# A streaming encoder layer on 8 cores: weights laid out in blocks, cast in one DMA each, scratch stores spread over three tiles, sample tokens worked beside the first and the last tile

## The reference, cut to what matters

```python
def trunk_layer(x, ..., cache_k, cache_v):
    h = rms_norm(x, n_pre_mix)
    z = h @ w_in                                   # 1024 x 5632
    q, k, v, zg, ga, gb = jnp.split(z, offs, axis=-1)
    a = attn_prompt(q, k, v, sinks)                # own 64-frame chunk + 2 before
    # or attn_sample(q, k, v, cache_k, cache_v, sinks)
    u, gv = jnp.split(jax.nn.gelu(zg), 2, axis=-1)
    gv = layer_norm(gv, ln_g, ln_b)
    bm = spatial_gate(u, gv, w_s, b_s)             # u * (tril(w_s) gv + b_s), 128 positions
    merged = sigmoid(ga) * (a @ w_attn_proj) + sigmoid(gb) * (bm @ w_gmlp_proj)
    x = x + rms_norm(merged @ w_out, n_post_mix)
    h2 = rms_norm(x, n_pre_ffn)
    g, up = jnp.split(h2 @ w_ffn_in, 2, axis=-1)   # 1024 x 5632
    x = x + rms_norm((silu(g) * up) @ w_ffn_out, n_post_ffn)
    return x, new_k, new_v, gv
```

## Time and profile before

| what | value |
|---|---|
| three runs, us | 4579.6, 4606.01, 5141.87 (median 4606.01) |
| profiled execution, us | 4594.15 |
| its span on the slowest core (core 5), us | 4592.5 |
| spans of the eight cores, us | 4560.1 to 4592.5 |
| granted clock, mean of a core | 0.969 to 0.971 |
| busy: PE, DVE, ACT, POOL | 91%, 45%, 40%, 25% |
| DMA queues: SyncE's (q1), GpSimd's (q0) | 605.81 MB, 95.31 MB (as written) |

### The profile page before, as it was taken

One profiled execution on the slowest core, in us unless ns is written; L12 is line 12 of the kernel. 1 busy time (PEld: TensorE's weight loads), 2 busy tenths in 40 slices (PEclk: granted clock), 3 DMA queues, 4 the chain that ended last, 5 costly groups with the idle time before them and its releaser, 6 DMA issues.

```text
span 4592.5 us, 64392 instructions; the slowest of 8 cores (4560.1 to 4592.5 us)
## 1 busy us (share of the span) xinstructions
PE 4193.3 (91%) x21528; PEld 1887.5 (41%) x21528; DVE 2054.6 (45%) x2957; ACT 1848.6 (40%) x3525; POOL 1166.0 (25%) x1225
## 2 busy tenths in 40 slices
PE   2549899989999999999999999999999999999895
PEld 1214344434444444444444444444444444444343
DVE  1425445445454445445354445445454545445322
ACT  1515335243443526343353525344353525344231
POOL 1111022222223222232323222232323223232322
PEclk8779999989999999999999999999999999999997
DMA  6749953515435353533535343533535353543357
GB/s 120 152 84 201 209 187 120 181 63 187 160 121 187 135 168 140 178 130 125 187 112 197 133 173 138 179 129 127 188 111 198 131 179 129 173 137 131 133 184 263
DMA packets 168453, 709.43 MB, mean 154 GB/s; under 512 B 31073, under 2 KB 76129, under 8 KB 98498
## 3 DMA queue, kind: packets, MB, share of 16 engines
q1 hardware_dynamic: 87314, 605.81, 38.2%
q0 software_dynamic: 79088, 95.31, 10.0%
q10 hardware_dynamic: 1728, 4.20, 0.3%
HBM read 670.39 MB, written 69.99 MB: 161 GB/s over the span
## 4 chain that ended last, share of the span: by engine, by line
PE 73%; DMA 12%; DVE 6%; issue 4%; POOL 3%; ACT 2%; DVEq 0%; ACTq 0%; POOLq 0%; SPq 0%
PE ps L314 72%; DMA ring<-w_in 3%; DVE tmpf L342 3%; DMA ring<-wfi 2%; DMA yp<-tmpf 2%; DMA ring<-wap 2%; DVE hst L342 2%; POOL stt L331 1%; PE ps L482 1%; DVE xt L331 1%; ACT junk L321 1%; POOL big L331 1%; DMA ring<-s_wfi 1%; DMA wsf<-w_s 0%; DVE stt L338 0%
## 5 line engine op out<-in xcount | busy, mean ns | idle before, releaser
L314 PE MATMUL ps<-big,ring 128*128 128x512 bf16 (+1 forms) x12784 | 2745.0, 371 | 194.1 <-DMA ring<-w_in 51.2
L314 PEld LDWEIGHTS ps<-big,ring 128*128 128x128 bf16 x12784 | 1176.0, 99 | 1634.3 <-issue 344.6
L314 PE MATMUL ps<-ring,big 128*128 128x512 bf16 (+2 forms) x5476 | 1163.8, 371 | 24.0 <-POOL big L331 12.5
L331 POOL TENSOR_TENSOR big<-tmpf 128x512 bf16<-128x512 f32 (+1 forms) x480 | 603.8, 1258 | 1453.6 <-ACT tmpf L326 1152.1
L319 ACT ACTIVATE big<-ps 128x512 bf16<-128x512 f32 (+2 forms) x674 | 437.6, 658 | 916.0 <-PE ps L314 507.2
L314 PEld LDWEIGHTS ps<-ring,big 128*128 128x128 bf16 (+1 forms) x5476 | 531.9, 98 | 608.4 <-issue 47.1
L331 POOL TENSOR_TENSOR stt<-stt,negh 128x1 f32<-128x1 f32 (+1 forms) x297 | 226.9, 765 | 1297.7 <-DVE stt L335 913.7
L342 DVE SCALAR_TENSOR_TENSOR tmpf<-tmpf,ps 128x512 f32<-128x512 f32 (+1 forms) x374 | 245.7, 657 | 654.2 <-ACT tmpf L319 638.1
L319 ACT ACTIVATE y<-ps 64x512 bf16<-64x512 f32 (+2 forms) x1024 | 488.5, 478 | 54.0 <-ACT y L319 0.7
L321 ACT ACTIVATE junk<-ps 128x512 bf16<-128x512 f32 x260 | 155.1, 597 | 729.7 <-PE ps L314 722.3
L639 DVE RECIPROCAL dent<-dent 128x256 f32<-128x256 f32 (+1 forms) x264 | 441.8, 1693 | 8.3 <-DVE dent L331 0.5
(11 more groups left out here) (93 smaller groups left out, 1890.5 us busy)
## 6 DMA issues: line engine op xcount, KB each, us to landing
ring<-s_win SPq DMA_DIRECT2D x176, 1024.0 KB, 6.1
ring<-s_wfi SPq DMA_DIRECT2D x176, 1024.0 KB, 5.0
ring<-s_wfo SPq DMA_DIRECT2D x64, 1024.0 KB, 5.0
ring<-s_wap SPq DMA_DIRECT2D x32, 1024.0 KB, 10.0
ring<-s_wgp SPq DMA_DIRECT2D x32, 1024.0 KB, 10.8
ring<-s_wout SPq DMA_DIRECT2D x32, 1024.0 KB, 5.1
yp<-tmpf POOLq DMA_DIRECT2D x120, 256.0 KB, 9.0
xt<-xp POOLq DMA_DIRECT2D x52, 512.0 KB, 11.9
```

What stands on the lines that cost most here:

```text
L314: m.op(PE, lambda e: e.matmul(out, lhsT=lhsT, rhs=rhs, start=start, stop=stop), reads=reads, writes=[("ps", b)])
L331: m.op(eng, lambda e: e.tensor_tensor(out=out, in0=in0, in1=in1, op=op), reads=reads, writes=writes)
```

## The change

The host lays each weight out in blocks of [128, 8, 512] (with the head order of q and of wap's rows, and the g and u halves of wfi's blocks, already in place). A block is cast by one DMA, whose row for a partition is one run of 16 KB of f32. Scratch has one contiguous MB per block. A block is cast from f32 not only at its first use: `store_use` says at which use (0 is tile 0) the slot is stored as well, and only later uses load from scratch. The PX and YQ switch moves from the end of iteration 0 to that of iteration 2. The sample tile leaves the loop. Its own small buffers (`bigs`, `tmps`, `kTs`, `Vts`) let its qkv, u, gv and gates run beside tile 0's in the prologue, on the same ring slots (`smp["w"] = t["w"]`), and its merge, wout and feed-forward beside tile 15's. Constants are loaded in two parts, `consts_a` behind the first norm and `consts_b` in the middle of tile 0's u; w_s comes transposed from the host, so `setup_wmt` and `sample_w` are gone.

```diff
-        for h in range(16):
-            t, half = qperm(h)
-            cb, j = divmod(t, 4)
-            c0 = j * 128 + half * 64
-            cj(("s_win", cb), (A_, A_, slice(c0, c0 + 64)), wsrc(w_in, h * 64, 64))
...
         for cb in range(11):
+            reg(("s_win", cb), w_in[cb, :, :, :], s_win[cb, :, :, :], 1 + cb % 2)
+            reg(("s_wfi", cb), wfi[cb, :, :, :], s_wfi[cb, :, :, :], 1 if cb < 4 else 2)
         for cb in range(2):
+            reg(("s_wap", cb), wap[cb, :, :, :], s_wap[cb, :, :, :], 1)
+            reg(("s_wgp", cb), wgp[cb, :, :, :], s_wgp[cb, :, :, :], 1)
+            reg(("s_wout", cb), wout[cb, :, :, :], s_wout[cb, :, :, :], 1)
             for c, (k0, k1) in enumerate(FCH):
+                reg(("s_wfo", cb, c), wfo[cb, :, k0:k1, :], s_wfo[cb, :, k0:k1, :], 2)
...
-            if key not in converted:
-                converted.add(key)
-                for idx, in_ in conv_jobs[key]:
-                    m.dma(POOL, ("ring0", s), slot_v[idx], in_, writes=[("ring", s)])
-                m.dma(SP, ("cvst", key), blk_view[key], slot_v, reads=[("ring", s)], writes=[key])
+            n = uses.get(key, 0)
+            uses[key] = n + 1
+            if n <= store_use[key]:
+                m.dma(POOL, ("ring0", s), slot_v, f32_of[key], writes=[("ring", s)])
+                if n == store_use[key]:
+                    m.dma(SP, ("cvst", key), b16_of[key], slot_v, reads=[("ring", s)], writes=[key])
             else:
-                m.dma(SP, ("ring", s), slot_v, blk_view[key], reads=[key], writes=[("ring", s)])
+                m.dma(SP, ("ring", s), slot_v, b16_of[key], reads=[key], writes=[("ring", s)])
...
         for b in range(4):
             xload(SP, tiles[0], b)
+        m.dma(SP, ("c_g", 0), gS[:, 0, :], g_in[0][0:1, :].partition_broadcast(128), writes=[("gS", 0)])
+        xload(SP, smp, 0)
...
+        m.fence([POOL], [k for b in range(4) for k in xk(b)])
+        for s_ in range(2):
+            m.dma(POOL, ("c_ck", s_), ckb[:, s_, :], ck[s_, :, :], writes=[("ckb", s_)])
+            m.dma(POOL, ("c_cv", s_), Vc[:, s_, :], cv[s_, :, :], writes=[("Vc", s_)])
+        def consts_a():
+            m.fence([SP], BK(tiles[0], C_H, C_H + 8, (3,)))
+            m.dma(SP, "c_es", es[:], sinks[0:1, :].partition_broadcast(128), writes=["es"])
...
+        def consts_b():
+            m.fence([SP], BK(tiles[0], C_U, C_U + 4, ALLB))
+            for i in range(1, 4):
+                m.dma(SP, ("c_g", i), gS[:, i, :], g_in[i][0:1, :].partition_broadcast(128), writes=[("gS", i)])
+                act(gS[:, i, :], gS[:, i, :], AF.Copy, [("gS", i)], [("gS", i)], scale=32.0)
+            for b in range(4):
+                xload(SP, tiles[1], b)
...
+        both(qkv_units(t)[0:10], qkv_units(smp)[0:10], 10)
+        both(qkv_units(t)[10:], qkv_units(smp)[10:], 4)
...
+        both(u_units(t)[0:4], u_units(smp)[0:4], 4)
+        ev(now[0], consts_b)
+        both(u_units(t)[4:], u_units(smp)[4:], 4)
...
+            if fin:
+                for f in range(8):
+                    for second in (False, True):
+                        dense(merge_unit(smp, f, second), SC)
+                for n in range(2):
+                    dense(wout_unit(smp, 0, n), UNIT)
+                plan_post(smp, 0, now[0])
...
+            for c in range(13 if fin else 11):
+                if c < 11:
+                    ffn_col(t, c, UNIT)
+                if fin and c >= 2:
+                    ffn_col(smp, c - 2, SC)
-            if i == 0:
+            if i == 2:
                 ev(now[0] + 2.5 + UNIT, lambda: (PX.__setitem__(0, POOL), YQ.__setitem__(0, POOL)))
```

More of the change, by code:

```diff
@@ L391, in build_program @@
         ring_ctr = [0]
-        converted = set()
+        uses = {}
         def wload(key):
@@ L553, in attn_S @@
+                return fn
+            return out + [v_unit(b) for b in range(t["NB"])]
         def attn_S(t, n, b, tp, which):
@@ L989, in build_program @@
+        memset(POOL, tri[:], 1.0, ["tri"])
+        m.op(POOL, lambda e: e.affine_select(out=tri[:], in_=tri[:], pattern=[[1, 128]],
+                                             compare_op=ALU.is_ge, fill=0.0, base=0, channel_multiplier=-1),
+             reads=["tri"], writes=["tri"])
         memset(DVE, PT[:], 0.0, [("PT", i) for i in range(8)])
         memset(DVE, bsX[:], 0.0, ["bsX"])
-        for b in range(4):
-            xload(SP, tiles[1], b)
+        act(gS[:, 0, :], gS[:, 0, :], AF.Copy, [("gS", 0)], [("gS", 0)], scale=32.0)
@@ L1050, in build_program, with ffn_col @@
             s0 = now[0]
-            for c in range(11):
+            def ffn_col(t, c, cost):
                 for jj in range(2):
@@ L1117, in make_in_maps @@
     cv = f(inputs["cache_attn_v"])[0].reshape(16, 128, 256)
+    w_in = f(inputs["w_in"])[0]
+    heads = [0] * 16
+    for h in range(16):
+        c, half = qperm(h)
+        heads[2 * c + half] = h
+    cols = np.concatenate([np.arange(64 * h, 64 * h + 64) for h in heads])
+    w_in = np.concatenate([w_in[:, cols], w_in[:, 1024:]], axis=1)
+    wap = f(inputs["w_attn_proj"])[0][cols, :]
+    wfi = f(inputs["w_ffn_in"])[0]
+    wfi = np.concatenate([np.concatenate([wfi[:, 256 * i:256 * i + 256], wfi[:, DFF + 256 * i:DFF + 256 * i + 256]],
+                                         axis=1) for i in range(11)], axis=1)
+    blk = lambda w: np.ascontiguousarray(w.reshape(w.shape[0] // 128, 128, w.shape[1] // 512, 512).transpose(2, 1, 0, 3))
+    b_s = f(inputs["gmlp_b_s"])[0]
     shared = {
```

490 lines of the change are left out of this document (231 added, 259 removed).

## The result

The changed kernel takes 0.972 of the time of before, 95% interval 0.9652 to 0.9788: 4460.7 and 4466.4 us, about 130 us less. The forecast was 287 less, at 4307, and the measured time lies 81 to 86 us above the upper end of the range. The sign was right, and more than half of the forecast gain is missing.

What follows compares the result with a forecast made beforehand. PE bounds the middle tiles; the start, iterations 0 to 2 and end also wait, largely on DMAs. 4592.5 - 193.7 (start to tile 3's first merge) - 93.4 (end) = 4305.4, with 1.65 around the span 4307; range 4240 to 4380.

Steps and rivals of the forecast that it cites:

- cast rival: Two on a block's cast price: 5.4 to 6 us, kernel 4261 (0.17); or 7.9 us, kernel 4351 (0.20).
- M(3): DVE's first merge instruction of tile 3, start of the steady tiles; forecast at 973.7 us against 1167.4 before.
- The steady period: Tiles 3 to 14: no change from 260.24 us a tile, as the new scratch layout's loads are hidden.
- The end: First merge of tile 15 to the span's end: 208.8 us against 302.2, saving 93.4.
- stalls of small columns: At the end: if ACT and DVE stall with each small column of the sample, 10 to 15 us more.
- signs of being wrong: PE waits for w_in or wfo over 30 us in iteration 0, ACT's gS wait over 15, low prologue clock.
- M(0): DVE's first merge instruction of tile 0, ending the start: 31 + 76.6 + 18 + 19.5 + 1.8 + 16 = 163 us.
- this holds the DVE and ACT mode as well ... both hidden in the mean: Iterations 0 to 2: the late switch's DVE products and ACT table loads fit within the 15, 10 and 5 us.
- the 30 for iterations 0 to 2: Time added to three steady periods of 260.24 us for uneven DMA demand and the DVE and ACT mode.
- the cover by six slots: Iterations 0 to 2: six slots give some 41 us of cover; 15, 10 and 5 us stay uncovered.
- 8 and 8: Start: 8 us for ACT's wait for three broadcasts in consts_b, 8 for ACT being tight; bounds together 0 and 30.
- The prediction's last rival: Start stalls return through consts_a and consts_b, 60 us, kernel 4351; chance within 0.13, shared with steady drift and the end.

Runs made afterwards that it cites:

- e3: Changed kernel with each block cast once and stored at its first use instead of spread over later tiles, the switch still late; 4451 us.
- e4: e3 with the PX and YQ switch back at the end of iteration 0; 4388 to 4389 us, ratio 0.954 to before.
- e1: Changed kernel with the host layout transposed, so that a cast has 1024 rows of 2 KB instead of rows of 16 KB; 4450 us.
- e2: Changed kernel without the stores of y for tiles 0 and 1, that part of the output not written; 4440 us.
- e15: Changed kernel with the gains' scalings behind the prologue, gates and attention first, and small constants loaded ahead of the casts; 4418, 4422 us, ratio 0.962.
- e8: Kernel before with only the host's block layout and one cast DMA for each block; 4480 to 4488 us, ratio 0.975 to before.

## Why the prediction failed, by its own steps

**Right.** The norm is through at 30.8 (said: 31). Casts cost what was said: at 14 to 62 us GpSimd's queue has 97.8% of the 16 engines' time for 7.74 MB written, 0.978 x 48 / 7.38 blocks = 6.4 us a block, and 0.692 x 275 / 30.7 = 6.2 later, where I took 6.8; neither cast rival decides. By the Trainium skill (DMA: Bandwidth & Descriptors, section Bandwidth) it would be 5.9 as an estimate, which is near. Up to M(3) PE's waits hold none for the ring. The steady period is 259.5 against 260.2, inside what cores differ by. The end is 218.6 for 208.8, a term mis-sized by 10: PE is busy 190 there and idle 28, where the stalls and the tail of the sum have 16, and the prediction named 10 to 15 for stalls of small columns but left it out. Of the signs of being wrong only the clock came: 0.84 from 31 us to M(0). ACT's waits for the three gains were 8.9 us in all, and PE did not wait for the ring, so the signs watched weights and gains, and the miss came from elsewhere.

**Wrong, first: "this holds the DVE and ACT mode as well ... both hidden in the mean".** It is not hidden. By e3 and e4 it is 44 us in iterations 1 and 2. Iteration 0 shows 14 to 20 above a steady tile in all kernels that store first; in e3 PE waits there for the same evictions as in iteration 1 and for no weights, so I count it with the mode, but no run has the mode off in iteration 0. That is some 60 us, where the 30 for iterations 0 to 2 were to hold this and the casts. I had compared busy times, 123 of 260 on DVE, when the mode's cost is a chain: statistics, table load, Sqrt, reciprocal, product, transposes. The move of the switch had thus been costed at nothing, by a comparison of busy times.

**Wrong, second: the cover by six slots.** 15, 10 and 5 us were to hold all unevenness. Spread stores cost 33 us over e3 on core 5 (873.6 against 840.7 for three iterations; 40 on core 4). The path was not weights coming late, which I looked for, but y stores that wait behind long packets (e1, e2). The 60 (e3 over three periods) and the 33 (the changed kernel over e3) add up to the 93 measured against 30 forecast, as they must; 42 of the 60 are in iterations 1 and 2, where an edit shows them, and the 18 of iteration 0 are argued.

**Wrong, third: M(0)'s stalls, "8 and 8".** 62 us were missing: from 31 us to M(0) PE was idle for 53.2 us where the sum has 16, and busy for 140.7 where it has 115.9. The prediction's last rival, stalls from consts_a and consts_b of 60 us with a chance within 0.13, came nearest. The three edits give back 41 of the 62 on the changed kernel: gains 11, ACT's table swaps and the order 11, small constants 19. The mechanism for the first two was named in the sum, with 8 each; the third was not, since the loads in `consts_a` were counted as DMA time and not as waits of DVE in front of the eviction of kT. Of the 21 left, 12 are PE's busy time: 127.8 where the terms of the sum make 115.9. They were priced at the row of full clock, but the stage had a mean granted clock of 0.90 in e15 (127.8 x 0.90 = 115) and 0.84 in the changed kernel, between the two levels of 1.2 and 2.4 GHz. The row for that stood in front of me: 121 us of PE for 536 matmuls at 0.83. The other 9 are idle time of PE; in e15 its longest waits behind the norm are for DVE's `gvn`, 14.9 us in all. No run takes these away.

**The sum of the change.** The forecast gave the start 99 and iteration 0 80 us as the work of all parts together. By e8 the block layout alone does 47.5 and 78 of them (28.5 and 81 on core 4), and spreading the stores, which was meant as relief for the queue, loses against storing at once: by 33 us itself, and by the 44 of the switch that it forces back.

## What to carry to other kernels

Here an engine that does elementwise work and issues transfers held casts behind products that needed those casts, and it cost 314 us: look at what is queued behind each, and if the transfers are spread out, so is the time for which that engine is lost to other work. Cost a mode by the chain of small steps at a norm, not by how busy its engines are. And a small load read by an in-order engine has the price of everything behind it on that engine, so load it ahead of the bulk or read it late; an experiment that wins time in front of such a wait shows little until the wait is gone.
